# The first projection tiles of a two-layer block multiply x·norm1_g without its row factor, which is applied when they are read from PSUM

## The reference, cut to what matters

```python
def rms_norm(x, g):
    xf = x.astype(jnp.float32)
    y = xf * lax.rsqrt(jnp.mean(xf * xf, axis=-1, keepdims=True) + EPS)
    return (y * g.astype(jnp.float32)).astype(x.dtype)
...
h = rms_norm(x, norm1_g[i])
proj = jnp.einsum('bsd,de->bse', h, w_in[i])
q, k, v, z, a, b, hp, cb, cc, ch = jnp.split(proj, offsets[1:], axis=-1)
# gated_deltanet:
qkv = jax.nn.silu(causal_dwconv(jnp.concatenate([q, k, v], axis=-1), conv_w))
q = l2norm(q.reshape(hs)); k = l2norm(k.reshape(hs))
beta = jax.nn.sigmoid(b)
g = -jnp.exp(a_log) * jax.nn.softplus(a + dt_bias)
o = chunk_gated_delta_rule(q, k, v, g, beta)   # cumulative sums of g: the decay rows
```

## Time and profile before

| | |
|---|---|
| median of 3 runs | 1407.06 us (1404.26 to 1408.09) |
| the profiled execution | 1408.91 us, its span 1406.8 us |
| TensorE busy | 1329.6 us, 95% of the span |
| VectorE, ScalarE, GpSimd busy | 609.3, 528.6, 574.2 us |
| share of the chain that ended last | PE 86%, DVE 8%, ACT 3% |
| mean granted TensorE clock | 0.976 |

### The profile page before, as it was taken

One profiled execution on the slowest core, in us unless ns is written; L12 is line 12 of the kernel. 1 busy time (PEld: TensorE's weight loads), 2 busy tenths in 40 slices (PEclk: granted clock), 3 DMA queues, 4 the chain that ended last, 5 costly groups with the idle time before them and its releaser, 6 DMA issues.

```text
span 1406.8 us, 15946 instructions
## 1 busy us (share of the span) xinstructions
PE 1329.6 (95%) x6257; PEld 1057.0 (75%) x6257; DVE 609.3 (43%) x839; ACT 528.6 (38%) x809; POOL 574.2 (41%) x431
## 2 busy tenths in 40 slices
PE   4899989999999999999999999889989999999996
PEld 3677778867888888888887875555668888888885
DVE  6637744245212621121266625556568523415123
ACT  4566333355222222221265343455436322323232
POOL 3343351234555554544454433211227545444440
PEclk7899999999999999999999999999999999999998
DMA  5213210123333333332342322101124333333321
GB/s 172 61 50 85 61 31 16 55 80 90 98 104 91 105 90 105 91 103 81 101 106 61 97 60 52 45 31 31 46 60 120 90 101 94 98 98 92 103 60 60
DMA packets 211361, 111.67 MB, mean 79 GB/s; under 512 B 16140, under 2 KB 209496, under 8 KB 211288
## 3 DMA queue, kind: packets, MB, share of 16 engines
q1 hardware_dynamic: 210488, 109.81, 27.5%
q10 hardware_dynamic: 672, 0.79, 0.2%
q0 software_dynamic: 128, 0.07, 0.0%
HBM read 108.55 MB, written 2.10 MB: 79 GB/s over the span
## 4 chain that ended last, share of the span: by engine, by line
PE 86%; DVE 8%; ACT 3%; issue 1%; POOL 1%; DMA 0%; DVEq 0%; ACTq 0%; SPq 0%
PE bank L1832 22%; PE bank L1834 22%; PE bank L1833 22%; PE aux L2040 1%; PE bank L1880 1%; PE aux L2056 1%; PE bank L1882 1%; PE bank L1881 1%; PE bank L1094 1%; PE aux L1110 1%; PE aux L2069 1%; PE aux L1035 1%; PE bank L972 1%; PE aux L1023 1%; PE aux L1832 1%
## 5 line engine op out<-in xcount | busy, mean ns | idle before, releaser
L1790 POOL TENSOR_TENSOR wl<-raw,wh 128x512 fp32r<-128x512 f32 (+1 forms) x404 | 552.2, 1389 | 769.1 <-ACT wh L2163 769.0
L1832 PE MATMUL bank<-ah,wh 128*128 128x512 f32 x912 | 364.1, 399 | 0.0
L1834 PE MATMUL bank<-al,wh 128*128 128x512 f32 x912 | 356.4, 391 | 0.0
L1833 PE MATMUL bank<-ah,wl 128*128 128x512 f32 x912 | 356.3, 391 | 0.0
L2163 ACT CAST wh<-raw 128x1024 fp32r<-128x1024 f32 (+1 forms) x202 | 209.1, 1038 | 369.2 <-PE bank L1834 359.4
L1832 PEld LDWEIGHTS bank<-ah,wh 128*128 128x128 f32 x912 | 171.9, 189 | 39.7 <-issue 5.3
L1834 PEld LDWEIGHTS bank<-al,wh 128*128 128x128 f32 x912 | 171.9, 189 | 36.3
L1833 PEld LDWEIGHTS bank<-ah,wl 128*128 128x128 f32 x912 | 172.1, 189 | 35.4 <-issue 1.2
L1832 PE MATMUL bank<-yh,wh 128*128 128x512 f32 x496 | 193.8, 391 | 0.1
L1834 PE MATMUL bank<-yl,wh 128*128 128x512 f32 x496 | 193.1, 389 | 0.0
L1833 PE MATMUL bank<-yh,wl 128*128 128x512 f32 x496 | 193.0, 389 | 0.0
(11 more groups left out here) (407 smaller groups left out, 1610.4 us busy)
## 6 DMA issues: line engine op xcount, KB each, us to landing
raw<-in_w_up SPq DMA_DIRECT2D x54, 512.0 KB, 3.9
raw<-in_w_down SPq DMA_DIRECT2D x48, 512.0 KB, 4.1
raw<-in_w_in SPq DMA_DIRECT2D x40, 512.0 KB, 3.9
raw<-in_w_gate SPq DMA_DIRECT2D x22, 512.0 KB, 3.8
raw<-in_w_out SPq DMA_DIRECT2D x16, 512.0 KB, 4.0
raw<-in_ple_gate SPq DMA_DIRECT2D x8, 512.0 KB, 4.1
raw<-in_w_down SPq DMA_DIRECT2D x8, 384.0 KB, 3.4
xtok<-in_x SPq DMA_DIRECT2D x4, 512.0 KB, 5.2
```

What stands on the lines that cost most here:

```text
L1790: nc.gpsimd.tensor_tensor(wl[pl.slot[b]][:, half], raw[b % RAW][:, half], wh[pl.slot[b]][:, half].bitcast(F32), ALU.subtract).then_inc(wl_ ...
L1832: nc.tensor.matmul(ps, h[:, c:c + P], mh[:, k, :], start=(n == 0), stop=False)
L1833: nc.tensor.matmul(ps, l[:, c:c + P], mh[:, k, :], start=False, stop=False)
L1834: last = nc.tensor.matmul(ps, h[:, c:c + P], ml[:, k, :], start=False, stop=(n == nk - 1))
```

## The change

- Two new operands, `zh` and `zl`, are the rounded and the remaining part of x·norm1_g, without r. They lie where qT, qg, bv and kd lie later. Tiles "ab", k0, k1 and k2 (the three k tiles are now called "kn") multiply these; k3 and all later tiles multiply `ah`, `al` as before.
- x is turned into six PSUM banks at first (24 transposes); slices 6 and 7 follow within the first pair of tiles, when banks are free (`turn_late`). `zh` is written by ScalarE and `zl` by VectorE, both straight from PSUM; the copies of x to SBUF come in between.
- The row sums of squares come from the loaded chunks: ScalarE squares each chunk of 128 tokens by 1024 features with an accumulated output (`rcol`), then Ln and Exp on 4 columns. VectorE multiplies the identity by these columns, and TensorE spreads the result over the partitions by four matmuls with ones (`factor_row`), copied to `rstd` by ScalarE.
- The factor is applied as the tiles are read: VectorE multiplies "ab" and the three "kn" tiles by `rstd` from PSUM (`keys`). ScalarE multiplies the last tap from the SBUF copy.
- norm1_g is loaded ahead of x and turned first. The first pair takes its wl·zh matmuls two slices at a time from slice 4 on.
- The spreading of the decay rows and its eight small turns move behind k3 and q0; the work on `ah`, `al`, the decay inputs and the `keys` is interleaved on VectorE and ScalarE.
- The buffers from kT on start at an address in step with wh0 (mod 256 bytes).

```diff
-            pe.wait_ge(ident_loaded, 16)
+            pe.wait_ge(first_loaded, 32)
+            nc.tensor.transpose(bank[0][:, 0:KD], prow[0:KD, 0, :], ident[0:KD, 0:KD]).then_inc(par_ps, 1)
             for c in range(NC):
                 pe.wait_ge(x_loaded[c], 16)
-                for k in range(KD):
...
+                for k in range(6):
+                    last = nc.tensor.transpose(x_psum(k)[:, c * P:(c + 1) * P], xtok[:, c, k * P:(k + 1) * P], ident)
...
+            def turn_late(k):
+
+                pe.wait_ge(x_ready, k - 5)
+                for c in range(NC):
+                    last = nc.tensor.transpose(x_psum(k)[:, c * P:(c + 1) * P], xtok[:, c, k * P:(k + 1) * P], ident)
+                last.then_inc(xt_ps, 1)
+
+            def factor_row():
+
+                pe.wait_ge(fills_set, 1)
+                pe.wait_ge(diag_ready, 1)
+                pe.wait_ge(x_ready, 3)
+                for c in range(NC):
+                    last = nc.tensor.matmul(aux[2][:, c * P:(c + 1) * P], ones[:, :], h32[:, 0, c * P:(c + 1) * P],
+                                            start=True, stop=True)
+                last.then_inc(ssq_done, 1)
+
+            def first_pair():
...
+                low = ((), (), (), (), (0, 4), (1, 5), (2, 6), (3, 7))
+                pe.wait_ge(par_ready, 1)
+                pe.wait_ge(wh_ready, 2)
+                for k in range(KD):
+                    pe.wait_ge(al_ready, k + 1)
+                    if k == 4:
+                        pe.wait_ge(wl_ready, 4)
+                    for u in range(2):
...
+                    if k in (1, 2):
+                        turn_late(k + 5)
+                    if k == 3:
+                        factor_row()
+
+            first_pair()
+            pe.wait_ge(x_ready, 5)
+            gemm("kn", 1, mov=(zh, zl))
+            pe.wait_ge(consts_loaded, 16 * len(PARAMS))
             pe.wait_ge(x_ready, KD)
-            pe.wait_ge(gain_loaded, 16)
-            nc.tensor.transpose(aux[2][:, 0:KD], prow[0:KD, 0, :], ident[0:KD, 0:KD]).then_inc(par_ps, 1)
-            ssq(0)
-
-            gemm_pair(("ab", 0), ("k", 0), (al_ready, 0))
...
-            gemm("k", 1)
-            gemm("k", 2)
+            gemm("kn", 2, mov=(zh, zl))
+            gemm("k", 3, ready=(al_ready, KD * F_NORM1))
+            gemm("q", 0)
             pe.wait_ge(par_ready, 2)
...
-            gemm("k", 3)
-            gemm("q", 0)
             gemm("q", 1)
             gemm("q", 2)
```

On ScalarE:

```diff
+            for c in range(NC):
+                act.wait_ge(x_loaded[c], 16)
+                link(nc.scalar.activation(sq[:, :, :].rearrange("p a n -> p (a n)"), xtok[:, c, :], ACT.Square,
+                                          accum_out=rcol[:, c:c + 1]))
+            act.wait_ge(fills_set, 2)
+            link(nc.scalar.activation(rcol[:, :], rcol[:, :], ACT.Ln, bias=eps[:, 0:1], scale=1.0 / D))
+            nc.scalar.activation(rcol[:, :], rcol[:, :], ACT.Exp, scale=-0.5).then_inc(rcol_ready, 1)
+            split(-1, most=1)
+            act.wait_ge(par_ready, 1)
             for k in range(KD):
-                act.wait_ge(x_ready, k + 1)
-                square(0, k, x[:, k, :])
-            split(-1)
-            act.wait_ge(eps_set, 1)
-            norm(0)
+                act.wait_ge(xt_ps, k + 1)
+                nc.scalar.activation(zh[:, k, :], x_psum(k)[:, :], ACT.Copy, scale=g_of("norm1_g", k)).then_inc(
+                    ah_ready, 1)
+                if k in (0, 2):
+                    split(-1, most=1)
+            act.wait_ge(ssq_done, 1)
+            nc.scalar.copy(rstd[:, :], aux[2][:, :]).then_inc(rstd_ready, 1)
...
+                if kind == "kn":
+                    tile("kn", h)
+                    evacuated(act, "kn", h)
+                    act.wait_ge(par_ready, 2)
+                    nc.scalar.activation(cc[j % 2][:, :], craw[j % 2][:, 3:3 + T], ACT.Copy,
+                                         scale=tap).then_inc(last_tap, 1)
+                    return
```

On VectorE:

```diff
-            for k in range(KD):
-                dve.wait_ge(xt_ps, k + 1)
-                nc.vector.tensor_copy(x[:, k, :], (bank + aux)[k][:, :]).then_inc(x_ready, 1)
-                if k > 3:
-                    add_square(0, k - 3)
...
+            def x_low(k):
+
+                dve.wait_ge(ah_ready, k + 1)
+                nc.vector.scalar_tensor_tensor(zl[:, k, :], x_psum(k)[:, :], g_of("norm1_g", k),
+                                               zh[:, k, :].bitcast(F32), ALU.mult, ALU.subtract).then_inc(al_ready, 1)
...
+            def keys(j):
+
+                ps = tile("kn", j)
+                if j >= 2:
+                    dve.wait_ge(conv_done, j - 1)
+                freed(nc.vector.tensor_tensor(craw[j % 2][:, 3:3 + T], ps, rstd[:, :], ALU.mult))
+
+            keys(0)
+            keys(1)
```

More of the change, by code:

```diff
@@ L626, in build @@
         MIX1_ORDER = [4, 5, 6, 7, 0, 1, 2, 3]
-        HEADS = [("k", h) for h in range(H)] + [("q", h) for h in range(H)] + [("v", h) for h in range(H)]
+        HEADS = [("kn", h) for h in range(3)] + [("k", 3)] + [("q", h) for h in range(H)] + [("v", h) for h in range(H)]
         INV_PAIR = 2 * LEVELS
@@ L701, in parameters @@
         def parameters(sp):
-            for name, rows in PARAMS:
+            for name, rows in PARAMS[1:]:
                 second = PCOL[name] >= PSPLIT
@@ new lines, in x_copy @@
+            def x_copy(k):
+                nc.vector.tensor_copy(x[:, k, :], x_psum(k)[:, :]).then_inc(x_ready, 1)
+            x_low(0)
+            x_copy(0)
+            x_low(1)
+            x_copy(1)
+            dve.wait_ge(rcol_ready, 1)
+            for c in range(NC):
+                i = nc.vector.tensor_scalar(h32[:, 0, c * P:(c + 1) * P], ident, rcol[:, c:c + 1], None, ALU.mult)
+            i.then_inc(diag_ready, 1)
+            x_low(2)
+            x_copy(2)
+            x_low(3)
@@ new lines, in _, with normed_slice @@
+            x_low(4)
+            x_copy(3)
+            x_low(5)
+            x_copy(4)
+            x_low(6)
+            x_copy(5)
+            x_low(7)
+            x_copy(6)
+            x_copy(7)
+            dve.wait_ge(x_ready, KD)
+            dve.wait_ge(rstd_ready, 1)
+            def normed_slice(k):
+                if k >= 3:
+                    dve.wait_ge(al_ready, KD * F_NORM1 + k - 2)
+                nc.vector.scalar_tensor_tensor(h32[:, k % 3, :], x[:, k, :], g_of("norm1_g", k), rstd[:, :],
+                                               ALU.mult, ALU.mult).then_inc(h32_ready, 1)
+                if k > 0:
+                    lower(F_NORM1, k - 1, k - 1, h32[:, (k - 1) % 3, :])
@@ L2481, in _ @@
+            for k in range(3):
+                normed_slice(k)
             ps = tile("ab", 0)
             dve.wait_ge(cols_loaded, 48)
-            freed(nc.vector.tensor_scalar(gab[:, :], ps[0:8, :], cols[0:8, 0:1], None, ALU.add))
+            link(nc.vector.tensor_tensor(gab[:, :], ps[0:8, :], rstd[0:8, :], ALU.mult))
+            freed(nc.vector.tensor_scalar(gab[:, :], gab[:, :], cols[0:8, 0:1], None, ALU.add))
             evacuated(dve, "ab", 0)
@@ L2530, in _ @@
             conv(0)
+            keys(2)
             conv(1)
```

113 lines of the change are left out of this document (65 added, 48 removed).

## The result

The changed kernel takes 1398.64 us (median of 9 runs, 1395.43 to 1402.79); the kernel before, run beside it, 1409.87 (9 runs, 1404.26 to 1410.52). The ratio is 0.9929, 95% interval 0.9912 to 0.9945: faster by 0.7%, about 11 us. I had predicted 1388, a range of 1384 to 1396 and a gain of 19.2: the sign was right, the size was not, and the time is outside the range.

The account below looks back on a forecast made before the run. TensorE, busy 95% of the span, bounds the kernel; only idle and half-clock stretches can be won. Timeline terms put the head sums' end at 74.9 against 94.1, gaining 19.2 us: 1389.7 from the profiled 1408.9, median 1388, range 1384 to 1396.

Parts of the forecast that it names:

- pair starts: First matmul of the first pair of tiles, after squares, Ln, Exp, casts and zh: 14.1 us, against 27.6 before.
- pair ends: First pair of tiles: 11.0 us of matmuls, 0.9 transposes, 0.9 factor row, 2.7 lost to half clock; ends at 29.6.
- k3 starts: First tile on ah/al, waiting 1.4 us for GpSimd's half of its weights behind ScalarE's cast; runs 42.3 to 47.8.
- rows start: Spreading of the decay rows, behind q0 and ScalarE's tap of k2: starts at 53.6, with no slack left.
- q1 starts: Tile behind the decay rows, which are bound by ScalarE's eight evacuations and take 6.2 us: 59.8.
- the point: First matmul behind the head sums, where the worked-out timelines end: 74.9 us against 94.09, a gain of 19.2.
- VectorE keeps up: During the first pair: 16 operations from PSUM at about 0.65 and four small ones put VectorE's last x copy at 24.8.
- q0's chain: q0's cast stands behind the k0 tap, waiting for parameters (45.0); tap 0.7, cast 1.0, GpSimd 1.3: q0 at 48.0.
- My rival of the late vector chain: VectorE and ScalarE late at k3 and the rows, pair's gain standing: gain 10 to 16, 1391 to 1397; chance 0.25.
- the half clock there: In the first pair: 5.5 us at half clock, as before the change, losing 2.7 us.
- the end of the rows' 6.4 us wait: At the decay rows: two more tiles in front eat TensorE's 6.4 us wait for ScalarE's evacuation.
- nothing lost behind the point: Behind the head sums: ScalarE's extra lag of about 2.7 us is absorbed, so the gain is not given back.

Follow-up runs that it names:

- the two repairs: Changed kernel with VectorE's products with r ahead of the first zl, and q0's weight cast ahead of the tap waiting for the parameters: 1392.45 us, ratio 0.9893.
- The early cast: Changed kernel with ScalarE casting q0's weights directly behind k3's, ahead of the k0 tap that waits for the parameters: 1395.26 us, ratio 0.9902.
- With the clock kept at the start: Changed kernel with products with r first, q0's cast early, and thirty transposes filling TensorE's wait ahead of the first pair: 1390.19 us, ratio 0.9877.
- the repeat: The changed kernel itself run again, unaltered, as the measure for the other runs: 1397.6 us, ratio 0.9919 to the kernel before.
- both repairs and the fillers: Changed kernel with products first, early q0 cast, thirty transposes ahead of the pair, and two transposes behind each decay row: 1395.15 us, ratio 0.991.
- interleaving: Changed kernel with the eight decay rows spread one after each slice of q1 instead of all ahead of q1: 1402.86 us, ratio 0.9947.

## Why the prediction was wrong

Point by point, my time, the changed kernel's, and that with the two repairs:

| | predicted | changed | two repairs |
|---|---|---|---|
| pair starts | 14.1 | 14.50 | 14.27 |
| pair ends | 29.6 | 31.53 | 28.67 |
| k3 starts | 42.3 | 43.79 | 40.75 |
| q0 starts | 48.0 | 51.66 | 46.35 |
| rows start | 53.6 | 57.37 | 51.88 |
| q1 starts | 59.8 | 64.42 | 60.05 |
| the point | 74.9 | 80.51 | 77.20 |

**The step that failed first** is in the sentence that begins "VectorE keeps up: 16 operations from PSUM at about 0.65 and four small ones". The four small ones are the products with r. Worked back from the 24.8, I took them at about 0.3 each, and they took 3.96 together in GpSimd's company; last x copy at 27.8 for 24.8. That is 1.5 us of TensorE at the pair's end, beside 0.4 from its start. Run by itself, this one order change gave back 2.0 us there. I had weighed the rule for it and read only half: the Trainium skill, SBUF — State Buffer, Who interferes with whom, frees an instruction with at most one SBUF input only outside VectorE's two-port modes, and lists `tensor_scalar`, the operation of these products, among those that can enter such a mode and then contend with GpSimd, the later of the two being blocked. I left that condition out, and applied only what it says of instructions with two SBUF inputs. The trace agrees with both halves here: a product took 0.28 alone and 1.30 beside GpSimd, a tap, which has two SBUF inputs, 0.77 and up to 1.37.

**Mis-sized in the same way:** q0's chain. I had k3's and q0's place in it right (k3 waits 0.7 for `wl`, for my 1.4; ScalarE idle for `par` with the cast behind), but charged 1.2 for decay passes that took 2.5, and 1.3 for a half of `wl` that took 2.3. Along the chain that set q0's start, the last `al` was 1.5 late (42.15 for 40.6), the stretch from there to the parameters about 1.0 longer, and the stretch from the tap to the end of GpSimd's half 1.2; on TensorE's own line, of q0's 3.7 us of delay 1.9 came from the pair and 1.8 arose behind it. My rival of the late vector chain, with a chance of 0.25, comes nearest: its gain of 10 to 16 at the point holds the measured 13.6. But it let the pair's gain stand and lost its time at k3 and at the rows, and its 1391 to 1397 doesn't hold 1398.64 either; the losses arose in the pair and at q0. The early cast alone removed q0's wait.

**The clock in the rows** was the term that I left out. I took 6.2 us for the rows, from the 6.60 that they and their turns had taken at half clock, and full clock for q1; they took 7.05, and q1's first 3.1 us ran at half. Together with all else behind the rows' start that is 1.8 us at the point. The two repairs confirm it: with them the rows start 1.7 us ahead of my time and the point is 2.3 behind it, so 4.0 us go in between, with waits of 1.1 for ScalarE and half clock from 55.3 to 65.5. With the clock kept at the start the kernel reaches 74.94, but by other terms than mine: the pair ends 1.9 earlier (27.70), and the rows lose it.

Sum at the point: 0.4+1.5+1.8+0.1+1.8 = 5.6 us, all of the 80.51-74.9; the 0.1 is q0's end to the rows' start (5.71 for 5.6). The other 5 us of the 10.6 between 1388 and 1398.64 are no step of that profile: the profiled run was 3.2 below the median, and I had subtracted 1.8 for a median of before that proved to be 1409.87. What the 3.2 are, the repeat shows, whose profiled run (1399.67) is nearer to the median: the same waits, longer half clock, and the point 2.7 later. In such a run the clock, with 1.8 and 2.7 us, is the largest single term of the miss.

**Right:** the start of the pair, the half clock there, a wait of k3 for `wl`, the end of the rows' 6.4 us wait, the square of a chunk (1.06 us and 0.19 for the read of its sum, 1.25 estimated), and nothing lost behind the point, within the spread told above. **Wrong in weight:** I had not priced the two parts apart. The run with the rows put back shows that the earlier pair alone gives about 1.7 us, and that the other 9.6 come only when the rows move too; the move without the earlier pair I did not try.

**Open:** why the clock falls in the rows. Idle time of TensorE there isn't needed for it, since it falls too where there is none: with both repairs and the fillers it fell at 56.3, TensorE having been busy since 40. Idle time ahead may still bring it down elsewhere: in three of the traces it fell at about the end of q0's wait of 2.1 us (50.1, 53.0 and 53.0), in four others with the same wait it did not. The stretches of rows have in common the matmuls on 8 partitions, which is not shown to be the cause: in one run the same mix of them with q1's slices stayed at full clock. I did not try rows on all partitions.

## What to carry to other kernels

Before costing a small VectorE instruction, look which GpSimd instruction runs beside it: between SBUF tiles each may wait for one of GpSimd's, so its price can be that of the neighbour (1.30 here), not its own (0.28), and moving it ahead of the neighbour cost nothing here. When a wait goes, work out the next stretch at both clock levels, since the same program lands on either. A wait spread thin over one engine still holds everything queued behind it on the engine that serves it: interleaving cost 4 to 5 us, though it removed all of TensorE's waits in the rows.

## What the hardware showed that I had not expected

- Four 128x128 products in SBUF: 0.87 us alone, 3.96 beside GpSimd; four scans over 8x128: 1.36 alone, 3.39 beside it; taps 0.77 each alone and up to 1.37 beside it.
- Thirty transposes of a constant in a wait of 3.9 us kept the granted clock at 1.00 from 13 to 19 us, where it was 0.50 without them.
- A busy TensorE can stay at 1.2 GHz: 18.00 of 18 us busy, clock 0.50, in matmuls on 8 partitions mixed with full ones; the like stretch of another kernel ran at 1.00.
- The clock can fall without a pause: it did at 56.3 us, with TensorE busy for 15.97 us from 40 to 56.
